# Two-layer decoder trunk on one core: the per-layer embedding stage (PLE) with x copied first, a gate pass by row blocks, the last gate tile in two parts, squares on ACT and four stores

## The reference

```
for i in range(DEPTH):
    h = _rmsnorm(x, norm_mix[i])
    ...
    x = x + y
    h = _rmsnorm(x, norm_moe[i])
    x = x + _hier_moe(h, moe_w_group[i], moe_b_group[i], moe_w_expert[i], moe_b_expert[i],
                      moe_w_gate[i], moe_w_up[i], moe_w_down[i])
    gate = jax.nn.sigmoid(_rmsnorm(x, norm_ple[i]) @ ple_w_gate[i])
    x = x + (p[i] @ ple_w[i]) * gate
return _rmsnorm(x, norm_final)
```

## Time and profile before

| What | us |
|---|---|
| median of three runs | 1388.43 (1388.11 to 1392.02) |
| the profiled execution's own time | 1391.07 |
| its span in the profile | 1389.2 |
| PE busy in the span | 1057.8 (76%) |
| DVE busy | 457.7 (33%) |
| ACT busy | 292.8 (21%) |
| the chain that ended last | DMA 49%, PE 44%, DVE 3%, issue 2%, ACT 1% |
| PLE stage of layer 0, from the last scatter to the first latent product | 748.38 to 784.25 |
| PLE stage of layer 1, from the last scatter to the end | 1348.74 to 1389.2 |

### The profile page before, as it was taken

One profiled execution on the slowest core, in us unless ns is written; L12 is line 12 of the kernel. 1 busy time (PEld: TensorE's weight loads), 2 busy tenths in 40 slices (PEclk: granted clock), 3 DMA queues, 4 the chain that ended last, 5 costly groups with the idle time before them and its releaser, 6 DMA issues.

```text
span 1389.2 us, 30964 instructions
## 1 busy us (share of the span) xinstructions
PE 1057.8 (76%) x13756; PEld 821.9 (59%) x13756; DVE 457.7 (33%) x1017; ACT 292.8 (21%) x555; POOL 9.2 (1%) x19
## 2 busy tenths in 40 slices
PE   6999999988666667667667989976666666666667
PEld 6999999865545445444445645555444444444446
DVE  6545555552212111111114666521121211121127
ACT  5433444220100000000004444310000000000016
POOL 1000000000000000000000000000000000000000
PEclk9999999999988877988898999998888888898899
DMA  9996540699999999999999740499999999999980
GB/s 272 310 239 175 159 119 0 267 367 426 425 426 426 427 426 426 426 426 426 426 427 393 276 177 1 148 425 427 426 426 426 427 426 426 426 426 427 426 365 35
DMA packets 113483, 469.97 MB, mean 338 GB/s; under 512 B 4656, under 2 KB 78512, under 8 KB 88528
## 3 DMA queue, kind: packets, MB, share of 16 engines
q1 hardware_dynamic: 112672, 465.78, 83.7%
q0 software_dynamic: 688, 2.28, 0.4%
HBM read 467.00 MB, written 1.05 MB: 337 GB/s over the span
## 4 chain that ended last, share of the span: by engine, by line
DMA 49%; PE 44%; DVE 3%; issue 2%; ACT 1%; DVEq 0%; SPq 0%; ACTq 0%
DMA ring<-moe_w_down 33%; DMA ring<-moe_w_up 8%; PE ps L1608 6%; DMA ring<-ple_w_gate 5%; PE ps L1379 5%; PE ps L1380 5%; PE ps L1381 5%; PE ps L1623 4%; PE ps L1695 3%; DMA ring<-moe_w_gate 3%; PE ps L1493 2%; PE ps L1653 2%; PE ps L1514 1%; PE ps L1443 1%; PE ps L1419 1%
## 5 line engine op out<-in xcount | busy, mean ns | idle before, releaser
L1608 PE MATMUL ps<-ring,scr 128*32 128x128 f32 x8192 | 291.2, 302 | 161.3 <-DMA ring<-moe_w_up 103.8
L1608 PEld LDWEIGHTS ps<-ring,scr 128*32 128x32 f32 x8192 | 252.6, 122 | 202.2 <-DMA ring<-moe_w_up 115.0
L1623 PE MATMUL ps<-ring,scr 128*32 128x256 f32 x2048 | 170.0, 485 | 114.8 <-DMA ring<-moe_w_down 100.6
L1623 PEld LDWEIGHTS ps<-ring,scr 128*32 128x32 f32 x2048 | 83.5, 134 | 183.3 <-issue 103.7
L1131 DVE TENSOR_TENSOR scr<-scr,ps 128x128 f32<-128x128 f32 x64 | 23.8, 372 | 445.9 <-PE ps L1608 445.9
L716 ACT COPY scr<-ps 32x256 f32<-32x256 f32 x128 | 46.8, 366 | 557.2 <-PE ps L1623 556.5
L1144 DVE COPY scr<-ps 32x256 f32<-32x256 f32 x128 | 53.3, 416 | 239.0 <-PE ps L1623 238.2
L1379 PE MATMUL ps<-hT_hi,w_qk_hi 128*128 128x256 f32 x368 | 104.4, 284 | 0.0
L1381 PE MATMUL ps<-hT_hi,w_qk_lo 128*128 128x256 f32 x368 | 103.7, 282 | 0.0
L1380 PE MATMUL ps<-hT_lo,w_qk_hi 128*128 128x256 f32 x368 | 103.6, 281 | 0.0
L1653 PE MATMUL ps<-scr 128*128 128x512 f32 x128 | 63.1, 639 | 15.5 <-DVE scr L1144 15.5
(11 more groups left out here) (239 smaller groups left out, 1182.3 us busy)
## 6 DMA issues: line engine op xcount, KB each, us to landing
ring<-moe_w_gate SPq DMA_DIRECT2D x64, 2048.0 KB, 36.0
ring<-moe_w_up SPq DMA_DIRECT2D x64, 2048.0 KB, 36.4
ring<-moe_w_down SPq DMA_DIRECT2D x64, 2048.0 KB, 36.3
ring<-dsa_w_in SPq DMA_DIRECT2D x72, 512.0 KB, 6.8
ring<-ple_w_gate SPq DMA_DIRECT2D x4, 2048.0 KB, 37.3
ring<-dsa_w_out SPq DMA_DIRECT2D x2, 2048.0 KB, 13.6
ring<-mla_w_out SPq DMA_DIRECT2D x2, 2048.0 KB, 24.5
x_sb<-ple_w SPq DMA_DIRECT2D x2, 1024.0 KB, 6.2
```

The costliest lines, as they stand in the source:

```text
L1608: mm = pe.matmul(bank(b)[CW * q:CW * q + CW, 0:P], xT[:, k, :], tile(t + j, KD, FF)[:, k, P * q:P * q + P], start=(k == 0), stop=(k == KD ...
L1623: mm = pe.matmul(bank(6)[CW * q:CW * q + CW, 0:T], e_hT[:, CW * j:CW * j + CW], tile(t + 2, FF // P, D)[:, j, T * q:T * q + T], start=(j = ...
```

## The change

It changes the PLE stage of both layers, and the end of layer 1.

- ACT and DVE copy x first. ACT's order becomes: copy tile 0, two rows of `g_hi` (`EARLY` = 2), copy tile 1, the four casts to `hT_hi`, the other six rows, the second half's eight. DVE makes all low rows of the first half after `hT_lo`. ACT no longer waits for `scattered` ahead of all this.
- PE's first gate half goes by `k`: high by high for both tiles as soon as row `k` of `g_hi` is there, and low by high two rows behind.
- The last tile and half, (1,1), is made as two parts of 256 columns in banks 3 and 2 (`gate_part`), with 48 matmuls of 256 columns in place of 24 of 512; `pg_ready` and `sig_ready` count five in a layer (`GATES`). In layer 0 the transposes of tile 0's scaled rows (`turn_rows(3, 0)`) stand between the two parts.
- Squares of the first halves move from DVE to ACT, behind the first three sigmoids. The square of tile 1's second half moves from ACT to DVE.
- DVE's order at the end becomes: add (0,0), (1,0), (0,1); root and finish of tile 0; the two parts of (1,1); the last square; root and finish of tile 1.
- In layer 1 the final scaling is split: DVE multiplies the first half by the final gain early (`final_gain`), and ACT scales it by the root (`final`, a Copy with a scale); DVE does the second half. SP stores each half of each tile, four stores of 256 KB.

The core of the diff:

```diff
-EARLY = 5
+EARLY = 2
+GATES = 5
+PART = 256
...
             for c in range(TC):
-                sp.wait_ge(S("final_ready"), c + 1)
-                sp.dma_start(out[0, c * P:(c + 1) * P, :], x_sb[:, c, :]).then_inc(S("stored"), 16)
-            sp.wait_ge(S("stored"), 16 * TC)
+                for n in range(2):
+                    sp.wait_ge(S("final_d" if n else "final_a"), c + 1)
+                    sp.dma_start(out[0, c * P:(c + 1) * P, 512 * n:512 * n + 512], x_sb[:, c, 512 * n:512 * n + 512]
+                                 ).then_inc(S("stored"), 16)
+            sp.wait_ge(S("stored"), 32 * TC)
...
-                act.wait_ge(S("scattered"), (NGRP + 1) * l + NGRP)
+                take_x(0)
                 high_gate(0, range(EARLY))
-                take_x(0)
-                high_gate(0, range(EARLY, KD))
                 take_x(1)
                 for c in range(TC):
                     for b in range(2):
                         act.wait_ge(S("hT_turned"), 4 * i + 2 * c + b + 1)
                         act.copy(hT_hi[:, c, 4 * b:4 * b + 4, :], bank(4 + 2 * c + b, 4, P)).then_inc(S("hT_high"), 1)
+                high_gate(0, range(EARLY, KD))
                 high_gate(1, range(KD))
...
                 for c, n in ((0, 0), (1, 0), (0, 1)):
                     sigmoid(c, n)
+                i = 3 * l + 3
+                for c in range(TC):
+                    wait_x(act, i, c, 0)
+                    act.activation(junk_pd[c], x_sb[:, c, 0:512], ACT.Square, accum_out=ss[:, c, 0:1]).then_inc(S("sq_d"), 1)
                 table(ACT.Sqrt)
-                norm_chunk(3 * l + 3, 0)
-                sigmoid(1, 1)
+                norm_chunk(i, 0)
+                table(ACT.Sigmoid)
+                for h in range(2):
+                    act.wait_ge(S("pg_ready"), GATES * l + 4 + h)
+                    act.activation(p_sig[:, 1, 512 + PART * h:512 + PART * h + PART], bank(3 - h)[:, 0:PART], ACT.Sigmoid,
+                                   scale=rstd[:, 1:2]).then_inc(S("sig_ready"), 1)
                 table(ACT.Sqrt)
-                norm_chunk(3 * l + 3, 1)
+                if l == 1:
+                    final(0)
+                act.wait_ge(S("var_ready"), TC * i + 2)
+                act.activation(root[:, 1:2], root[:, 1:2], ACT.Sqrt, scale=1.0 / D).then_inc(S("root_ready"), 1)
...
+                for k in range(EARLY, KD):
+                    for c in range(TC):
+                        high_by_high(c, k)
+                    low_by_high(k - EARLY)
...
+                high_by_low(0, 1)
+                gate_part(0)
+                if l == 0:
+                    turn_rows(3, 0)
+                gate_part(1)
```

More of the change, by code:

```diff
@@ L731, in experts, with final @@
                     act.wait_ge(S(f"o_down{l}"), NE + 1)
+            def final(c):
+                act.wait_ge(S("x_gained"), c + 1)
+                act.wait_ge(S("rstd_ready"), 6 * TC + c + 1)
+                act.activation(x_sb[:, c, 0:512], p_w[:, c, 0:512], ACT.Copy, scale=rstd[:, c:c + 1]
+                               ).then_inc(S("final_a"), 1)
             def ple(l):
@@ L1215, in ple @@
                                           ALU.subtract).then_inc(S("hT_low"), 1)
-                low_gate(0, range(EARLY - 1, KD))
+                low_gate(0, range(KD))
                 for c in range(TC):
@@ new lines, in gate_part @@
+                def gate_part(h):
+                    if h == 1:
+                        pe.wait_ge(S("sig_ready"), GATES * l + 2)
+                    cols = slice(PART * h, PART * h + PART)
+                    for x_k, w in ((hT_hi, g_hi), (hT_lo, g_hi), (hT_hi, g_lo[l])):
+                        for k in range(KD):
+                            x_1 = x_k[:, 1, k, :] if x_k is hT_hi else x_k[:, k, P:2 * P]
+                            mm = pe.matmul(bank(3 - h)[:, 0:PART], x_1, w[1][:, k, cols], start=(x_k is hT_hi and w is g_hi and k == 0),
+                                           stop=(w is not g_hi and k == KD - 1))
+                    mm.then_inc(S("pg_ready"), 1)
@@ new lines, in high_by_high, with low_by_high, high_by_low @@
+                def high_by_high(c, k):
+                    if c == 0:
+                        pe.wait_ge(S("g_high"), 2 * KD * l + k + 1)
+                    pe.wait_ge(S("hT_high"), high + 2 * c + k // 4 + 1)
+                    gate(c, 0, k, hT_hi, g_hi[0], first=(k == 0))
+                def low_by_high(k):
+                    for c in range(TC):
+                        pe.wait_ge(S("hT_low"), low + 2 * c + k // 4 + 1)
+                        gate(c, 0, k, hT_lo, g_hi[0])
+                def high_by_low(c, n):
+                    for k in range(KD):
+                        if c == 0:
+                            pe.wait_ge(S("g_low"), 2 * KD * l + KD * n + k + 1)
+                        mm = gate(c, n, k, hT_hi, g_lo[l][n], last=(k == KD - 1))
+                    mm.then_inc(S("pg_ready"), 1)
@@ new lines, in ple @@
+                for c in range(TC):
+                    for k in range(EARLY):
+                        high_by_high(c, k)
+                for k in range(EARLY, KD):
+                    for c in range(TC):
+                        high_by_high(c, k)
+                    low_by_high(k - EARLY)
+                for k in range(KD - EARLY, KD):
+                    low_by_high(k)
+                for c in range(TC):
+                    high_by_low(c, 0)
+                pe.wait_ge(S("g_high"), 2 * KD * l + 2 * KD)
@@ L1728, in _ @@
+                for k in range(KD):
+                    gate(0, 1, k, hT_hi, g_hi[1], first=(k == 0))
+                for k in range(KD):
+                    gate(0, 1, k, hT_lo, g_hi[1])
+                high_by_low(0, 1)
+                gate_part(0)
+                if l == 0:
+                    turn_rows(3, 0)
+                gate_part(1)
             experts(0)
```

76 lines of the change are left out of this document (36 added, 40 removed).

## The result

| What | before | after |
|---|---|---|
| median of 20 runs each, us | 1388.14 (1385.06 to 1393.21) | 1394.13 (1387.59 to 1396.90) |
| ratio, 95% interval | 1 | 1.0034 [1.0024, 1.0044] |
| the profiled execution's own time, its span | 1391.07, 1389.2 | 1396.09, 1394.2 |
| layer 0, last scatter to first latent product | 35.71 | 37.73 |
| layer 1, last scatter to the end of the span | 40.46 | 41.30 |

The kernel is slower, by 0.34% or 4.7 us by the ratio (the two medians lie 6.0 us apart); the forecast was 4.5 us faster. Of the 5.0 us between the two spans the two stages hold 2.9 (2.02 and 0.84).

What follows compares the result with a forecast made beforehand. Transfers were taken to bound the weight-streaming expert stages and a chain of waits the PLE stages between; 3.5 us (layer 1) plus 1.0 (layer 0) gave 4.5, from the median of 1388.43 to 1383.9 us, range 1381.6 to 1387.2.

Steps and rivals of the forecast that it cites:

- TensorE turns tile 0 right behind the scatter, and tile 1 after its copies: Start of layer 1's PLE stage: turns done at about 1354.3, not 1358.95, if the clock stays full.
- the idle time of 2.81 us: TensorE's idle time between layer 1's last scatter and the turns of x, read as a wait for DVE's copy.
- Rival E: Nothing changes: x is not what the turns wait for, or another wait takes its place; 1388.4 us, chance 0.04.
- the forecast of 1.0 us earlier: Layer 0's PLE stage: 2.6 us earlier at full clock, less 1.7 given back to a low clock after TensorE's idle time.
- The idle time before the scaled rows: Layer 0: TensorE idles some 3.5 us before turning tile 0's scaled rows, most likely bringing low clock.
- the forecast of 3.5 us earlier: End of layer 1: last scaling done at 1382.7 instead of 1386.18.
- the last sigmoids: End of layer 1: two short sigmoids at 1378.6 to 1379.3 wait for ACT's table loads; matmuls ready since 1377.4.
- the row at 1381.97: ACT table load near layer 1's end, the square starting after 1.46 us; taken as the price of each switch.
- rival C: Table loads cost 0.8 us more each; layer 1 gives back 2.4, layer 0 0.1; 1386.4 us, chance 0.11.
- A: Layer 0 keeps its clock or its idle time is shorter; 3.5 + 2.6 gives 1382.3 us, chance 0.15.
- B: Clock still falls at the first pass; layer 1 gains 2.7, layer 0 0.2; 1385.5 us, chance 0.14.
- D: Slower: low clock through the whole first pass in both layers, 9 lost against 4.5 won; 1392.9 us, chance 0.06.

Runs made afterwards that it cites:

- mix: Kernel with layer 0's stage in the old order and layer 1's as changed, TensorE's overflow block kept in place; 0.9979 of the kernel before, the same when repeated.
- a_short: Changed kernel with TensorE's If and value load kept, the body it steps over cut to two waits; 1.0005 of the kernel before.
- a_noblock: Changed kernel without TensorE's part of the overflow block (value load, If and loop) in both layers; 1.0014 of the kernel before.
- after_again: The changed kernel once more, unchanged, for a second profile; 1.0034 of the kernel before.
- tail_only: Kernel before with only the new end of the stage in both layers (two-part last tile, squares on ACT, split scaling, four stores); 1.0041 of the kernel before.
- b_else: Kernel before with TensorE's branch turned round: usual case in the If, overflow block and a copy of the stage in the Else; 1.0057 of the kernel before.
- mix_else: TensorE's branch turned round (usual case in the If, overflow in the Else), layer 0 in old order, layer 1 as changed; 1.0053 of the kernel before.
- b_straight: Kernel before with TensorE's If holding all the rest of the program, so the usual case meets no jump outside loops; 1.0016 of the kernel before.
- mix_straight: TensorE's If holding all the rest of the program, layer 0 in old order, layer 1 as changed; 0.9996 of the kernel before.

## Why the prediction was wrong

*The step that failed first: "TensorE turns tile 0 right behind the scatter, and tile 1 after its copies", which rested on reading the idle time of 2.81 us as a wait for DVE's copy, and on carrying it to layer 0.* In the kernel after, TensorE turned two blocks 3.54 us behind the start of the scatter, as forecast, and the other 14 at 7.85 in layer 0; in layer 1 it began at 5.99. For layer 1 the reading of the row was right: x ended the wait, and in mix, where the branch takes 0.36 us, all 16 turns begin at 3.54. There it failed on a branch that lasted 4.7 us in the changed kernel, which nothing in the trace of before shows. In layer 0 a second wait of nearly the same length lay beneath the first, and two hints stood there. 2 turns and 14 turns are separate rows with "0.23 <-issue" between them, at 755.82, 7.44 us behind the scatter; I spoke of its low clock and not of that word. And TensorE has an If between scatter and turns, which I didn't count among its instructions because it does nothing here. Rival E had the idea ("x is not what the turns wait for") with the wrong price: time that ACT and DVE lose while TensorE stands still comes back at the end, since DVE's low halves are the row that decides (20.72 us behind the scatter in layer 1, against 16.8 in mix).

*Layer 0, the forecast of 1.0 us earlier.* It was to be 34.7 us long. Without the stop it is (34.56 in a_short, 34.50 in a_noblock); with the stop of 3.4 to 3.9 us it was 37.7 to 38.1. The working there was loose by 0.4 us: from 774.2 to 778.2 are 4.0 us of idle time and not 3.5, and its terms end at 787.6 and not 787.2. The idle time before the scaled rows was 3.10 and 3.35, forecast 3.5, and the clock fell behind it in most profiles (the eight turns took 1.70 us in after_again and 1.97 in tail_only instead of 1.2), as said; in the profile of the kernel after itself they took 1.21, behind 3.10 us of idle time, and in tail_only 1.97 behind 2.71, so the length of the idle time, by which the earlier trace rows were read, does not sort the cases.

*Layer 1, the forecast of 3.5 us earlier.* It was to be 36.96 us long and is 37.32 where nothing stops TensorE. Step by step, in mix: DVE's second low halves end 22.15 us behind the scatter (forecast 22.06), the third pair of sums at 26.13 (26.26), the last sigmoids begin at 29.61, behind a table load, with the matmuls done 1.0 us before (29.86, and over a microsecond), the last scaling ends at 34.18 (33.96). From a table load to the next instruction it is 1.4 us, not 2.66: the reading of the row at 1381.97 held, rival C is out. The four stores end 3.1 us behind the last scaling, as two did.

*The size that was off in both: the kernel before itself.* The sum was made against stages of 35.7 and 40.5 us from one profiled execution. The second profile shows 33.05 and 38.18, and all other kernels with the old order in a layer have 31.8 to 33.6 and 38.6 to 38.9. The first profile had the low clock through layer 0's turns and first pass and through layer 1's turns, which not every run has; its own time was 2.6 us over the median, and the prediction noted that and then took the gain from it all the same. Against 71.2 us the forecast stages (71.7) are no gain at all, and a_short (71.9) measured 1.0005. In layer 0 even the forecast length of 34.7 is a loss against 33.05. So two errors of like size: 4.9 us of gain that was only the bad luck of one profile, and TensorE's stop on top. That the low clock fell into that profile was luck; taking its lengths as the base of the sum was not.

*Rivals.* A and B were about the low clock and had prices on the fast side (1382.3 and 1385.5); D did not come (the first pass ran at full clock in after_again and in mix's layer 1). The side that was called least likely came, by a mechanism that none of the rivals priced.

## What to carry to other kernels

Before work is moved ahead of an engine's wait, look in that same layer for a second wait under the first: a row broken in two with "issue" between, a branch row of microseconds, an If or a loop's end that stands there even when it is never entered. Instructions that are jumped over can cost microseconds, and the cheapest place seen here for such a jump was beside work that the other engines have to do anyway. What the jump costs may change with code far ahead of it, as the branch rows of layer 1 suggest. And when a stage holds stretches at low clock, take a second profile of the kernel before, or compare it with the same stage in the other layer, before its length becomes the base of a sum.

## What the runs showed of the hardware

- A taken branch of TensorE over 56 matmuls and a loop was followed in layer 0 by a stop in all ten profiles, until 7.2 to 7.9 us behind the scatter (3.4 to 3.9 us of idle time where x was early). In layer 1 the same source lines took 0.36 us in six profiles and 1.35 to 4.86 in four, 4.73 and 1.35 in two executions of the same kernel (idle time before the turns 2.29 us and none). Over two waits it took 0.24 to 0.35 us, and no stop followed.
- A branch that is not taken took 0.08 us (b_else, mix_else, b_straight, mix_straight).
- The position decides: a jump over the Else in the latent products (b_else) took 4.20 us, TensorE idled 3.62, and the stretch was 6.9 us longer, with the low clock (0.68) behind the stop.
- A scatter of eight matmuls took 3.70 us, or 5.4 to 6.0 where the granted clock was 0.59 to 0.68 through it (6 of the 34 stages profiled, in old and changed orders alike): a spread of 2 us ahead of a stage's work.
